# One Trainium2 core, a hybrid encoder layer with a routed mixture of experts: the unrolled expert steps are cut at another point of their cycle, and GpSimd's small root moves ahead of two of its DMA issues

## What is computed

```python
# h: tokens after the norm (T, 1024); 32 experts of width 256
order = jnp.argsort(flat_e)                    # the 2 T (token, expert) pairs, by expert
padded = (counts + 127) // 128 * 128           # each expert gets whole blocks of 128 rows
def run_block(args):                           # one block of 128 rows, one expert
    toks, e = args
    xb = h_pad[toks]
    return (silu(xb @ w_gate[e]) * (xb @ w_up[e])) @ w_down[e]
y = x + sum over a token's two experts of weight * its row of run_block
y = rms_norm(y, final_norm_g)
```

## Time and profile before

| what | value |
|---|---|
| median of three runs | 2767.61 us (2767.44, 2767.61, 2770.74) |
| the profiled execution, its own time | 2770.37 us |
| its span in the profile | 2768.6 us |
| granted PE clock, mean of the span | 0.993 |
| PE matmul busy | 2719.4 us, 98% of the span |
| DVE busy | 1916.3 us, 69% |
| ACT busy | 1453.6 us, 53% |
| POOL busy | 818.5 us, 30% |
| gate and up products (L1657) | x1296, 582.5 us, 592 ns of one |
| down products (L1676) | x320 and x320, 143.9 and 143.8 us |

### The profile page before, as it was taken

How to read it: one execution, slowest core, us unless ns; L and a number is a source line. 1 busy time by engine, 2 the same in 40 slices (tenths; PEclk the granted TensorE clock), 3 DMA queues, 4 the chain that set the end, 5 groups by cost and what they waited for, 6 DMA issues and landing times.

```text
span 2768.6 us, 38299 instructions
## 1 busy us (share of the span) xinstructions
PE 2719.4 (98%) x11649; PEld 1761.8 (64%) x11649; DVE 1916.3 (69%) x5154; ACT 1453.6 (53%) x3363; POOL 818.5 (30%) x1368
## 2 busy tenths in 40 slices
PE   8999999999999999999999999997999999999997
PEld 6777777767777777677767776773444444444443
DVE  5777777776777776767777767675666666666665
ACT  2445444554455445544554455444666666666665
POOL 1021112111211121112111211113565655656655
PEclk9999999999999999999999999998999999999999
DMA  8212211211121112111221121157888677778864
GB/s 322 94 62 77 62 46 47 77 62 46 47 76 62 47 47 77 61 47 47 72 66 46 46 76 62 50 197 281 302 285 293 239 264 267 280 256 294 319 212 145
DMA packets 109137, 377.90 MB, mean 136 GB/s; under 512 B 37201, under 2 KB 38866, under 8 KB 98930
## 3 DMA queue, kind: packets, MB, share of 16 engines
q1 hardware_dynamic: 48450, 236.13, 24.2%
q0 software_dynamic: 60480, 139.24, 15.0%
HBM read 326.14 MB, written 123.03 MB: 162 GB/s over the span
## 4 chain that ended last, share of the span: by engine, by line
PE 94%; DVE 2%; DMA 2%; issue 1%; ACT 1%; SPq 0%; POOL 0%; DVEq 0%; POOLq 0%; ACTq 0%
PE PB L369 24%; PE PB L1657 20%; PE PB L380 16%; PE PB L457 11%; PE SS L1676 5%; PE TB L1676 5%; PE YB L457 4%; PE YB L411 2%; DMA arena<-in_w_in 1%; PE SS L420 1%; PE SS L424 1%; PE TB L433 1%; PE YB L1667 1%; PE MB L402 1%; DVE xc L817 0%
## 5 line engine op out<-in xcount | busy, mean ns | idle before, releaser
L369 PE MATMUL PB<-arena,hT 128*128 128x512 f32 (+2 forms) x2112 | 727.7, 498 | 3.5 <-DVE x_res L937 2.2
L1657 PE MATMUL PB<-arena,hT 128*128 x1296 | 582.5, 592 | 0.0
L369 PEld LDWEIGHTS PB<-arena,hT 128*128 128x128 f32 x2112 | 397.7, 191 | 272.0 <-issue 222.4
L380 PE MATMUL PB<-hT,arena 128*128 128x128 f32 x4224 | 487.7, 277 | 4.7 <-DVE arena L1146 4.7
L380 PEld LDWEIGHTS PB<-hT,arena 128*128 128x128 f32 x4224 | 482.2, 193 | 8.6 <-issue 4.9
L1657 PEld LDWEIGHTS PB<-arena,hT 128*128 128x128 f32 x1296 | 240.2, 190 | 271.0 <-issue 271.0
L1183 POOL TENSOR_SCALAR rs<-sq 128x2 f32<-128x2 f32 (+1 forms) x66 | 14.0, 213 | 1238.5 <-ACT h L744 886.5
L457 PE MATMUL PB<-arena,tT 128*128 128x274 f32 (+1 forms) x1056 | 358.0, 493 | 0.3 <-ACT tT L638 0.3
L457 PEld LDWEIGHTS PB<-arena,tT 128*128 128x128 f32 x1056 | 195.6, 190 | 139.7 <-issue 120.5
L1787 DVE TENSOR_TENSOR gv<-ycat,PB 128x256 f32<-128x256 f32 x81 | 34.1, 421 | 288.9 <-ACT ycat L1739 288.9
L817 DVE SCALAR_TENSOR_TENSOR xc<-xT,cols,xc 128x128 f32<-128x128 f32 x792 | 216.8, 346 | 3.5
(11 more groups left out here) (292 smaller groups left out, 4204.1 us busy)
## 6 DMA issues: line engine op xcount, KB each, us to landing
arena<-in_w_expert SPq DMA_DIRECT2D x32, 2048.0 KB, 9.9
arena<-in_w_expert SPq DMA_DIRECT2D x32, 1024.0 KB, 6.5
h_rows<-h SPq DMA_DIRECT2D x34, 512.0 KB, 6.0
x_in<-in_x_rows SPq DMA_DIRECT2D x33, 512.0 KB, 4.3
hT<-in_x_cols SPq DMA_DIRECT2D x33, 512.0 KB, 3.7
x_res<-in_x_rows SPq DMA_DIRECT2D x33, 512.0 KB, 3.5
dec<-running_sums SPq DMA_DIRECT2D x33, 512.0 KB, 3.8
x_rows<-x_res SPq DMA_DIRECT2D x33, 512.0 KB, 5.2
```

Of the source, the lines that this page charges most:

```text
L369: mm = nc.tensor.matmul(out, hT[u][:, k, :], w_group(name)[:, k, :], start=k == 0, stop=k == KD - 1)
L380: mm = nc.tensor.matmul(PB[b][:, c * P:(c + 1) * P], w_block(name, c)[:, k, :], hT[u][:, k, :], start=k == 0, stop=k == KD - 1)
L1657: mm = nc.tensor.matmul(PB[u][:, :], hT[u][:, k, :], arena[:, bass.ds(slot + k * 2 * DE, 2 * DE)], start=k == 0, stop=k == KD - 1)
```

## The change

Four edits. PE's step now holds the product of block `b` (not `b + 1`) and hidden and down of block `b - 1`; the last hidden and down stand behind the loop, with the weight's place in `arena` taken from a cell that DVE fills (`final_slot`). ACT's step begins at `silu(b)`, DVE's at `gate(b)`. POOL's `gather` goes from third place in its step to last, behind the root, `earlier` and `store`. The number `2 used - 1` is read ahead of the loop (`but_one`) on ACT, DVE and POOL.

```diff
@@ pool_phase2
             def step(b):
                 if b > 0:
                     keep(b - 1)
                 residual(b + 1)
-                gather(b + AHEAD)
                 if b > 1:
                     pool.wait_ge(s["fin_sq"], b - 1)
                     root_of(b % 2, b - 1)
@@
                     store(b - 2)
+                gather(b + AHEAD)
@@
+            but_one = pool.value_load(misc[0:1, 4:5], min_val=2 * SURE - 1, max_val=2 * PAIRS - 1)
             used = over_pairs(pool, step)
-
-            last_n = (pool.value_load(misc[0:1, 4:5], min_val=2 * SURE - 1, max_val=2 * PAIRS - 1), 2 * used)
+            last_n = (but_one, 2 * used)
@@ pe_hidden, pe_down
-            pe.wait_ge(s["hb_ready"], b + 1)
-            pe.wait_ge(s["hbT_out"], b + 1)
@@ pe_phase2
             def step(b):
-                weights = pe_weights(pe, b + 1)
-                slot = entry(pe, TAB_SLOT, b, 0, SLOT_AT[2])
-                pe_gate_up(pe, b + 1, weights, 0, 4)
-                pe_hidden(pe, b)
-                pe_gate_up(pe, b + 1, weights, 4, KD)
-                pe_down(pe, b, slot)
+                if b == 0:
+                    pe_gate_up(pe, 0, weights0, 0, KD)
+                    pe.wait_ge(s["smp_new"], 8)
+                    return
+                weights = pe_weights(pe, b)
+                slot = entry(pe, TAB_SLOT, b - 1, 0, SLOT_AT[2])
+                pe_gate_up(pe, b, weights, 0, 4)
+                pe.wait_ge(s["hb_ready"], b)
+                pe_hidden(pe, b - 1)
+                pe_gate_up(pe, b, weights, 4, KD)
+                pe.wait_ge(s["hbT_out"], b)
+                pe_down(pe, b - 1, slot)
             pe_rows(pe, 0)
             pe_rows(pe, 1)
-            pe_gate_up(pe, 0, weights0, 0, KD)
-            pe.wait_ge(s["smp_new"], 8)
-            over_pairs(pe, step)
+            used = over_pairs(pe, step)
+
+            pe.wait_ge(s["hb_ready"], 2 * used)
+            pe_hidden(pe, 2 * SURE - 1)
+            slot = pe.value_load(final_slot, min_val=0, max_val=SLOT_AT[2])
+            pe.wait_ge(s["hbT_out"], 2 * used)
+            pe_down(pe, 2 * SURE - 1, slot)
@@ act_phase2
             def step(b):
+                silu(b)
+                move(b + 2, 0 if b == 0 else 6, 12)
                 hidden(b)
                 if b > 1:
                     squares(b % 2, f_buf[b % 2], b - 1)
                 move(b + 3, 0, 6)
-                silu(b + 1)
-                move(b + 3, 6, 12)
@@ dve_phase2
             def step(b):
+                if b % 2 and b // 2 >= SURE - 1:
+
+                    V.tensor_copy(final_i, last_i[:, b - 1:b + 1])
+                    V.tensor_copy(final_w, wt[:, b:b + 1])
+                    V.tensor_copy(final_slot, tab[0:1, TAB_SLOT, b:b + 1])
+                gate(b)
                 if b > 0:
                     dve.wait_ge(s["dn_full"], b + 1)
                     dve.wait_ge(x2_back[1 - b % 2], 16 * ((b + 1) // 2))
                     after(dve, first_kept, 16 * (b - 2))
                     weigh(1 - b % 2, wt[:, b - 1:b])
                 turn(b + 2)
-                gate(b + 1)
-                if b % 2 and b // 2 >= SURE - 1:
-
-                    V.tensor_copy(final_i, last_i[:, b - 1:b + 1])
-                    V.tensor_copy(final_w, wt[:, b:b + 1])
                 if b > 1:
                     norm(b % 2, f_buf[b % 2], b - 1)
```

More of the change, by code:

```diff
@@ L1407, in build @@
         final_w = mv[:, 0:1]
+        final_slot = lng_b[0:1, 2 * P + 2:2 * P + 3].bitcast(I32)
         final_i = lng_b[:, 2 * P:2 * P + 2].bitcast(I32)
@@ L1754, in step @@
                 move(b + 3, 0, 6)
-                silu(b + 1)
-                move(b + 3, 6, 12)
             rows0(0)
             rows0(1)
-            silu(0)
-            move(2, 0, 12)
+            but_one = act.value_load(misc[0:1, 4:5], min_val=2 * SURE - 1, max_val=2 * PAIRS - 1)
             used = over_pairs(act, step)
-            last_n = (act.value_load(misc[0:1, 4:5], min_val=2 * SURE - 1, max_val=2 * PAIRS - 1), 2 * used)
+            last_n = (but_one, 2 * used)
             squares(0, f_buf[0], last_n[0])
@@ L1827, in dve_phase2 @@
             rows1(1)
-            gate(0)
             dve.wait_ge(gf_loaded, 16)
+            but_one = dve.value_load(misc[0:1, 4:5], min_val=2 * SURE - 1, max_val=2 * PAIRS - 1)
             used = over_pairs(dve, step)
-            last_n = (dve.value_load(misc[0:1, 4:5], min_val=2 * SURE - 1, max_val=2 * PAIRS - 1), 2 * used)
+            last_n = (but_one, 2 * used)
             dve.wait_ge(s["first_added"], last_n[0])
```

## The result

| | before | changed |
|---|---|---|
| median | 2769.5 us (six runs) | 2829.7 us (six runs, 2800.6 to 2851.1) |
| ratio | | 1.0189, 95% interval 1.0159 to 1.0219 |
| span of the profiled execution | 2768.6 us | 2831.4 us |

The change makes the kernel about 2% slower: 60 us by the medians, 52 by the ratio. My forecast was 2766.7 us in a range to 2769.5, "the same": wrong. The runs of the changed kernel also lie 50 us apart, where those of before lie 4 apart.

What follows compares the result with a forecast made beforehand. The prediction took PE, busy throughout, to bound the loop, and DVE the tail. Terms of -1.3 (root), -0.7 (read) and +1.1 (beginning) sum to -0.9 us: 2767.61 becomes 2766.7 us, range 2763.8 to 2769.5.

Steps and rivals of the forecast that it cites:

- POOL's and DVE's new order inside the loop: Loop: `norm` straight behind `turn`, `gate` behind `norm` and `add_first`, gather issued 6 us later; costed at nothing.
- What bounds the loop: Loop: PE is busy for all 840 us, so only work taken off PE or a new PE wait changes time.
- Rival 4: Loop: `gate` hangs on POOL's root, and `earlier` beside `norm` takes 1.0 us more; 2776 us, chance 0.06.
- The root is 1.3 earlier in each step: Loop, on POOL: argument against the slower case, the root coming 1.3 us earlier in every step.
- The product that goes: PE: 80 gate and up products instead of 81, 6.87 us less work, not counted because the tail waits for DVE.
- The exit on PE's sequencer: PE's loop exit, between down(78) and the last transposes: takes 3.4 us, costed at nothing because PE's work covers it.
- The tail: Behind the loop: `weigh(79)` starts 2.0 us earlier, 1.3 from the earlier root and 0.7 from the read taken away.
- the exit on DVE: Tail: DVE's fetch of far code, kept at 3.0 us from the end of `add_first`.
- rival 1: Tail gains more: the pause leaves the root's path or DVE's exit counts from its branch; 2764.8 us, chance 0.22.
- The pause of 1.88 us: Tail, on POOL: idle time ahead of the last `residual`, taken to stay at the same place.
- another 1.6 us come off: Tail: further gain if POOL's pause falls elsewhere than ahead of the last `residual`.
- The beginning: Loop's start: PE reads `used` ahead of block 0's product and stands still 1.1 us, bounds 0.5 to 1.3.

Runs made afterwards that it cites:

- e2: The changed kernel with POOL's gather moved from last place to between the root and `earlier`: 2767.4 us, ratio 0.9992 to the kernel before.
- e6: e2's order, with PE reading the number of pairs behind the product of block 0 again, as the kernel before did: 2766.4 us, ratio 0.9989.
- e7: e1 with a further gather of 128 rows (512 KB) right ahead of `keep`, into a buffer nobody reads: 2839.0 us, ratio 1.0249.
- e1: The changed kernel with POOL's gather back in third place, ahead of the root: 2768.9 us, ratio 0.9996 to the kernel before.
- e4: The changed kernel, gather last, with DVE's `gate` ahead of `norm` again wherever the step has no branch behind it: 2799.8 us, ratio 1.0088.
- e5: The changed kernel, gather last, but from block 5 on each gather brings 32 of its 128 rows: 2769.5 us, ratio 1.0004.
- e8: e1 with a further gather of 32 rows (128 KB) right ahead of `keep`: 2775.1 us, ratio 1.0020.
- e3: The kernel before with POOL's gather moved to last in the step, DVE's order unchanged: 2783.1 us, ratio 1.0062.

## Why the prediction was wrong

The step that failed is the one on "POOL's and DVE's new order inside the loop", which I costed at nothing, and which, with the gather last, cost 52 to 60 us. For the moved gather I asked only when its own rows are needed, two steps later, and there I was right: in the change ACT waits for them twice, 1.5 us in sum. What I didn't ask is what is issued behind it. `keep` is, and `earlier` is held on POOL until `keep` has landed; the earlier trace rows showed that wait at 5.54 us, and I took it for one step of 80 near the edge. In the change such waits came to 260 us, and PE stood still for 48.1 behind them. The median from issue to landing of `keep` in the loop:

```profile
x_rows<-x_res,bc POOLq DMA_INDIRECT x79, 4.5
```

```profile
x_rows<-x_res,bc POOLq DMA_INDIRECT x78, 5.9
```

before, and after the change. The median alone doesn't tell a loss: it is 5.0 in e2 and 5.3 in e6, which lose nothing, and 5.3 in e7, which loses 70 us. The long landings with POOL's next issues behind them, as in the rows above, are what reaches the root.

- **What bounds the loop**: right for the kernel before, and it made the size of the error. With PE busy throughout, each gap of PE is the kernel's time, and the slower passes behind some of them come on top.
- **Rival 4, slower**: the chain root, `norm`, `add_first`, `gate`, `pe_hidden` was the right one, and so was what would show it. Its driver was wrong: not the port and the microsecond of `earlier` beside `norm`. In e2 the gather takes 2.06 us beside `norm` in its place, and nothing is lost:

```profile
2600.18 2.06 POOL L1554 DMA_INDIRECT xc<-h_rows,bc  x1 [0.23 <-issue]
```

  So its chance of 0.06 was put on too small a price, 2776 us for 2829.7. Its sum for POOL's own work was high too: rows 4 had the issue of 2.05 in it already, and a step of e7, with a sixth issue of 1.32 us and no wait, takes 9.77, so that of five issues takes about 8.4 and not 8.7 to 9.7. "The root is 1.3 earlier in each step" held only where `earlier` of the step before wasn't late.
- **The product that goes**: right. x1280 in place of x1296, PE's last down over 5.1 us before DVE weighed it (2812.31 and 2817.39). The exit on PE's sequencer took more than its 3.4 us, 5.2 after the change and 5.3 in e6, and the cover just held: the transposes followed the down product at once.

```profile
L1427 PEldq COMPARE_BRANCH  x1: 5317/5317/5317, 2734.7 to 2734.7; - x1
```

```profile
2740.35 0.38 PE L1667 MATMUL YB<-cst,gv 128*128 128x128 f32 x2
2741.29 3.69 PE L1675 MATMUL TB<-arena,xdt 128*128 x8 [0.56 <-ACT xdt L1753]
```

- **The tail**: 2.0 us forecast; the time from the end of down(78) to the end of the span was 27.5 before, 24.6 in e2, 24.3 in e6: 3 us less. The mis-sized term is the exit on DVE, taken as 3.0 us behind `add_first`. It was 1.0 in e6, about as rival 1 had it: 3.2 us from the branch at 2747.8. Why the same exit took 5.3 from the branch before the change isn't shown.

```profile
2748.82 1.22 DVE L1813 TENSOR_TENSOR arena<-x_res,arena 128x1024 f32<-128x1024 f32 x1
2751.04 0.06 DVE L1842 MEMSET spare<- 128x1 f32 x1 [1.00 <-DVE arena L1813]
```

  The pause of 1.88 us ahead of the last `residual` stayed where it was in e1, e2 and e6. In the change it did not: that `residual` was issued at 2811.41 after the usual 0.30, and POOL was idle for 2.20 us two issues later, ahead of `store`. Without a pause ahead of it the root ended 5.5 us behind the end of down(78), 8.6 before. That is the case which I had written down as "another 1.6 us come off". Some of the gain went back: the final add waited 0.92 us in e6 for the last `earlier`, which has the gather of an absent block ahead of it.
- **The beginning**: 1.1 us forecast, 0.54 in the change and 0.86 in e2. The read took 0.55 us in the change and 0.87 in e2, not 0.90. The start of the first product doesn't tell it: it came at 1902.04, since the first part ended 1.6 us earlier in that trace.

Without the gather in last place the forecast would have been met: e1 came out at 2768.9, e2 at 2767.4, both within the range. Part of that is luck. Against the kernel before as run beside them they are 0.8 and 2.3 us lower, for 0.9 forecast; the tail gave more than I had summed, and the median of the kernel before stood 2 us higher in these runs than in the three that I started from.

## What to carry to other kernels

When a transfer is moved, ask not only who waits for it but what is issued behind it on the same queue, and whether an engine in a cycle waits for that one's landing. An engine that issues DMAs in order and also waits for one of them can fall into a rhythm of its own, as POOL did here: the late issue sends the others out in a burst, and behind the burst the landing that it waits for is late again. Work that needs no waiting is better placed inside such a wait than behind it, as the gather in e1 and e2. A small computation on such an engine (here a root of 128 numbers) carries the delay to whoever reads it, so its readers are safer on their engine behind what the bounding engine needs; in e4 this took away about half of the loss.

## What the runs showed that I had not expected

- A gap of PE can cost more than itself: behind one of 2.10 us the next half product took 5.29 us for 3.60, at a mean granted clock of 0.67. That happened behind eight of the 20 gaps, and the length of the gap alone doesn't say which: behind one of 3.73 us the half took its 3.60.
- The exit from the unrolled loop to far code costs a sequencer 3.2 to 5.3 us, from the branch: 3.4 on PE before, 5.3 in e6; 5.3 on DVE before, 3.2 in e6.
- POOL pauses for about 1.88 us ahead of a DMA issue every 19 steps before the change, which is 95 issues of 128 rows, 12,160 rows. It goes by rows, not by issues: in e5, where one issue of five has 32 rows, 110 issues lie between two pauses, 11,968 rows, and in e8, where one of six has, 108 issues, 12,096 rows; the pause there is 2.5 us. With the gather last (the change, e3, e4) it stands two issues later than before. What POOL does there was not tried.
